# Hybrid attention encoder block: another order of stores, fetches and product parts around the routed units, and q's rotary copies issued by ScalarE

## The reference

```python
h = rmsnorm(x, norm_mix)
qa, ka, va, ga, cq, ckv, kr, gb = split(h @ w_in)
ya = window_attention(qa, ka, va, sink) * silu(ga)      # group A: banded, 8 heads
q = (rmsnorm(cq) @ w_uq)      # 8 heads of 64 plain + 32 rotary columns
kv = (rmsnorm(ckv) @ w_ukv)   # 8 heads of 64 (k) + 64 (v); one rotary k for all heads
yb = latent_attention(q, k, v) * silu(gb)               # group B: dense, 8 heads
out = final_norm * rmsnorm(x + concat(ya, yb) @ w_out)
```

## Time and profile before

| What | Value |
|---|---|
| Time, median of 3 runs | 622.18 us (621.98 to 623.96) |
| The profiled execution | 621.12 us, its span 619.3 us |
| PE busy | 601.3 us, 97% of the span |
| DVE busy | 446.7 us, 72% |
| ACT busy | 357.3 us, 58% |
| POOL busy | 288.4 us, 47% |
| Granted PE clock, mean | 0.997 of full speed |

### The profile page before, as it was taken

How to read it: one execution, slowest core, us unless ns; L and a number is a source line. 1 busy time by engine, 2 the same in 40 slices (tenths; PEclk the granted TensorE clock), 3 DMA queues, 4 the chain that set the end, 5 groups by cost and what they waited for, 6 DMA issues and landing times.

```text
span 619.3 us, 9200 instructions
## 1 busy us (share of the span) xinstructions
PE 601.3 (97%) x3092; PEld 485.7 (78%) x3092; DVE 446.7 (72%) x804; ACT 357.3 (58%) x762; POOL 288.4 (47%) x269
## 2 busy tenths in 40 slices
PE   8999999999999999999999999898989989999996
PEld 7888887888888888888887777676766767888885
DVE  5776653334445258999997899787887878799884
ACT  6645232313335147888785868677777778543563
POOL 4610705406657234354546626675666666320601
PEclk9999999999999999999999999999999999999999
DMA  6688458684767510101108656658567554499043
GB/s 248 187 278 246 125 151 288 203 272 135 256 209 275 172 35 1 35 7 29 26 22 236 165 135 170 162 135 211 129 168 191 128 147 146 156 355 350 3 152 121
DMA packets 70990, 100.00 MB, mean 161 GB/s; under 512 B 10072, under 2 KB 41824, under 8 KB 70944
## 3 DMA queue, kind: packets, MB, share of 16 engines
q1 hardware_dynamic: 70784, 99.15, 53.2%
q10 hardware_dynamic: 160, 0.27, 0.1%
HBM read 59.12 MB, written 30.57 MB: 145 GB/s over the span
## 4 chain that ended last, share of the span: by engine, by line
PE 77%; DMA 7%; DVE 5%; POOL 4%; SPq 3%; ACT 3%; issue 1%; POOLq 0%; ACTq 0%
PE ps L1817 17%; PE ps L1819 17%; PE ps L1818 17%; PE ps L2089 4%; DMA p_land<-probs_scratch 4%; PE ps L1989 3%; PE ps L2108 3%; PE ps L2109 2%; PE ps L2019 2%; PE ps L2024 2%; PE ps L1999 2%; PE ps L1976 2%; PE ps L1975 2%; PE ps L2000 1%; DVE pT_lo L1667 1%
## 5 line engine op out<-in xcount | busy, mean ns | idle before, releaser
L1667 DVE TENSOR_TENSOR pT_lo<-ps,pT_hi 128x512 fp32r<-128x512 f32 x106 | 71.7, 688 | 35.6 <-ACT pT_hi L1232 35.3
L1817 PE MATMUL ps<-hT_hi,w_hi 128*128 128x512 f32 x208 | 84.0, 404 | 0.0
L1219 ACT ACTIVATE p_b<-ps,stat 128x1024 f32<-128x1024 f32 x64 | 71.3, 1115 | 17.5 <-DVE stat L1644 16.6
L1819 PE MATMUL ps<-hT_hi,w_lo 128*128 128x512 f32 x208 | 81.4, 391 | 0.0
L1818 PE MATMUL ps<-hT_lo,w_hi 128*128 128x512 f32 x208 | 81.1, 390 | 0.0
L1644 DVE TENSOR_REDUCE stat<-ps 128x1 f32<-128x1024 f32 x64 | 76.7, 1214 | 2.2 <-PE ps L2039 2.0
L1232 ACT ACTIVATE pT_hi<-ps 128x512 fp32r<-128x512 f32 x106 | 62.3, 595 | 22.6 <-PE ps L2089 22.2
L2089 PE MATMUL ps<-ident,p_b 128*128 128x128 f32 x424 | 65.5, 278 | 2.0 <-DVE pT_lo L1667 1.9
L2089 PEld LDWEIGHTS ps<-ident,p_b 128*128 128x128 f32 x424 | 50.2, 141 | 22.0 <-DVE pT_lo L1667 6.5
L2108 PE MATMUL ps<-pT_hi,vB 128*128 128x512 f32 x128 | 55.8, 436 | 7.7 <-POOL pT_lo L924 7.7
L2109 PE MATMUL ps<-pT_lo,vB 128*128 128x512 f32 x128 | 51.0, 398 | 0.0
(11 more groups left out here) (222 smaller groups left out, 1482.8 us busy)
## 6 DMA issues: line engine op xcount, KB each, us to landing
w_raw<-w_in SPq DMA_DIRECT2D x13, 512.0 KB, 4.4
probs_scratch<-p_blk SPq DMA_DIRECT2D x44, 128.0 KB, 2.9
p_land<-probs_scratch SPq DMA_DIRECT2D x11, 512.0 KB, 4.7
x_in<-x SPq DMA_DIRECT2D x8, 512.0 KB, 3.8
wt_raw<-w_out SPq DMA_DIRECT2D x8, 512.0 KB, 4.3
t_scratch<-wt_hi SPq DMA_DIRECT2D x16, 256.0 KB, 2.6
t_scratch<-wt_lo SPq DMA_DIRECT2D x16, 256.0 KB, 2.8
q<-q_h SPq DMA_DIRECT2D x16, 256.0 KB, 4.0
```

The costliest lines, as they stand in the source:

```text
L1219: nc.scalar.activation(p_b[:, (U + 1) % 4, :], ps[:, b:b + 2, :].rearrange("p b c -> p (b c)"), ACT.Exp, bias=nm_b[:, U % 4:U % 4 + 1], ac ...
L1667: nc.vector.tensor_tensor(pT_lo[at_], ps[:, 4 + a, :].rearrange("p (k c) -> p k c", c=P), f(pT_hi[at_]), ALU.subtract).then_inc(s_bTl, 1)
L1817: nc.tensor.matmul(o, a_hi, b_hi, start=first, stop=False, skip_group_check=goes_on)
L1819: return nc.tensor.matmul(o, a_lo, b_hi, start=False, stop=last, skip_group_check=goes_on)
```

## The change

On SP, `copy_k_rows` goes ahead of `store_probs`, `copy_q_c` leaves SP for all heads from 2 on, and the fetch of the second routed unit of a head goes ahead of the fetch of reciprocals. On POOL, `routed_lo` goes ahead of the pieces, and the pieces of a head are taken as (0 and 3), 1, 2, 4, 5, none, none, 7. On ACT, `copy_q_c` is issued behind the first exponential of the pairs 10, 18, 26, 34, 42 and 50, and both parts of `routed_hi` stand behind the last `pT_b_hi` of the pair. On PE, the parts of the product move: part 0 to the end of the pair with U % 4 = 2, parts 1 and 2 in the next pair, part 3 to the very start of the pair after it.

```diff
@@ SP
                 copy_q_rows(h)
                 store_recips(2 * h - 3)
+                copy_k_rows(h)
                 store_probs(U)
                 fetch_recips(2 * h - 3)
-                copy_k_rows(h)
                 fetch_probs(U)
-                copy_q_c(h, s_dup)
                 if h + 1 < HEADS:
                     load_qk(h + 1)
                 store_recips(2 * h - 2)
                 if U + 4 in ROUTED:
                     store_probs(U + 4)
+                    fetch_probs(U + 4)
                 fetch_recips(2 * h - 2)
-                if U + 4 in ROUTED:
-                    fetch_probs(U + 4)
@@ POOL
             for U in range(B_UNITS + 8):
-                if U // NT + 1 < HEADS:
-                    split_piece(U // NT + 1, U % NT)
                 if U - 5 in ROUTED:
                     routed_lo(U - 5)
+                if U // NT + 1 < HEADS:
+                    for i in ((0, 3), (1,), (2,), (4,), (5,), (), (), (7,))[U % NT]:
+                        split_piece(U // NT + 1, i)
@@ ACT
+            def copy_q_c(h):
+                act.wait_ge(s_sph, 2 * h - 1)
+                for i in range(4):
+                    tiles = f(q_h[HD:QK, :]).rearrange("p (a b c) -> p a b c", b=2, c=P)[:, :, i // 2, :]
+                    nc.scalar.dma_start(f(q_c[h % 2][i * ROPE:(i + 1) * ROPE, :]).rearrange("p (a c) -> p a c", c=P),
+                                        tiles).then_inc(s_dup, 16)
...
                 exp_b(U)
+                if U >= NT and U % NT == 2 and U // NT + 1 < HEADS:
+                    copy_q_c(U // NT + 1)
                 if U >= 2:
                     pT_b_hi(U - 2, 1)
                     pT_b_hi(U - 1, 0)
                 exp_b(U + 1)
-                if U - 4 in ROUTED:
-                    routed_hi(U - 4, 0)
                 if U >= 2:
                     pT_b_hi(U - 1, 1)
                 if U - 4 in ROUTED:
-                    routed_hi(U - 4, 1)
+                    for a in range(2):
+                        routed_hi(U - 4, a)
@@ PE
+                G = (U - 6) // 4
+                if U >= 10 and U % 4 == 2:
+                    pv_b(G - 1, 3)
                 full_b(U)
                 rope_b(U)
                 gated_last(beside_b[1])
                 turn_b(U - 2, 0)
                 full_b(U + 1)
                 turn_b(U - 2, 1)
-                if U >= 6:
-                    pv_b((U - 6) // 4, (U - 6) % 4)
+                if U >= 6 and U % 4 == 0:
+                    pv_b(G, 1)
                 gated_last(beside_b[2])
                 turn_b(U - 1, 0)
-                if U >= 6:
-                    pv_b((U - 6) // 4, (U - 5) % 4)
+                if U >= 6 and U % 4 == 0:
+                    pv_b(G, 2)
                 gated_last(beside_b[3])
                 turn_b(U - 1, 1)
+                if U >= 6 and U % 4 == 2:
+                    pv_b(G, 0)
...
+                if U == B_UNITS:
+                    pv_b((U - 6) // 4, 1)
```

## The result

The changed kernel takes 639.87 us (median; 638.79 to 641.60) against 622.62 for the kernel before: a ratio of 1.029 with an interval of 1.026 to 1.032. It is slower by 17 us. The forecast was 631.5, in a range up to 636.5: the direction is right, about half of the size is missing, and the time lies outside the range. The profiled execution took 639.61 us, its span 637.8.

The account below looks back on a forecast made before the run. PE, busy 97% of the span, was taken as the bound. Terms +0.7 (pair 6), +4.7 (8 to 50), +2.2 (52 to 60), +1.7 (behind) gave +9.3 on 621.12: 630.4, forecast as a 631.5 us median; range 620.5 to 636.5.

Parts of the forecast that it names:

- The gain on the routed groups: Pairs 8 to 50: waits for routed units, queue order on SP and POOL, all go; worth 9.9 us.
- PE's order: Latent attention pairs: routed groups 0.5 us dearer, short 4.64, long 7.32; unrouted groups 1.7 dearer, 6.8 and 7.06.
- The chain of rotary product, maximum and two exponentials: Routed short pairs: chain sums to 4.64 us against 4.28 of PE work, so PE waits 0.36 in each.
- The last block of an unrouted short pair: On PE: waits 1.7 us for DVE to free its bank, starting 4.33 behind the rotary product.
- Where the issues begin: ACT, pairs 10 to 50 with copies: issues can't begin before the first exponential does, by the standalone wait's stamp.
- hidden copies: Rival, 20%: ACT's sequencer issues the copies ahead, so their 9.6 us vanish and the time is 621.9.
- What the issues cost: ACT, six pairs with copies: 2.65 us of issues, 1.10 covered by the exponential; 1.6 us per head, 9.6 in all.
- The clock: Rival, 9%: granted clock falls after PE's waits, 1.4 us beyond each wait; two to five falls make 634 to 638.
- the likeliest case: The forecast itself, 55%: copies, PE's order and gain sum to +9.3 us, giving 631.5.
- the rival in which the change doesn't do what it says: Rival, 6%: q_c's transfers make the stores of probabilities late; the old 7.7 us of waits return: 639.

Follow-up runs that it names:

- e2: Kernel before with only the new order of SP, POOL and ACT's routed copies; q_c copies on SP, PE's order as before: 614.53 us, ratio 0.989.
- e7: e2 with part 0 of a routed group behind the first block of the last unit instead of ahead of it: 612.08 us, ratio 0.984.
- e8: e2 with ACT's two routed conversions around the pair's last copy as before, so only SP's and POOL's orders are new: 612.32 us, ratio 0.984.
- e5: Changed kernel with ACT's four q_c issues directly ahead of the pair's first exponential instead of behind it: 623.62 us, ratio 1.002.
- e1: Changed kernel with the q_c copies back on SP, behind fetch_probs(U), and none on ACT: 620.74 us, ratio 1.000.
- e12: Changed kernel with PE's waits filled by 8 added products of zeros ahead of the rotary product that waits: 632.47 us, ratio 1.018.
- e9: Changed kernel with PE's six long waits filled by 16 products of zeros ahead of the rotary product that waits: 638.16 us, ratio 1.027.
- e11: Kernel before with the q_c copies moved to ACT and all else as before: 630.59 us, ratio 1.015.
- e10: e7 and e8 together: SP's and POOL's new orders, routed part 0 behind the last unit's first block, ACT's order as before: 612.24 us, ratio 0.985.
- e4: Changed kernel with PE's order as in the kernel before, the q_c copies staying on ACT: 622.7 us, ratio 1.003.
- e3: Kernel before with only the PE part of the change, its new order: 627.8 us, ratio 1.012.

## Where the prediction held, and the steps that failed

**The gain on the routed groups** holds: PE has no wait for POOL's pT_lo, and e2, with nothing else in it, is 1.1% faster. Of the 9.9 us put on it, e2 brings 5.6 (136.1 to 130.5) and e7 8.2; the rest goes with waits that the old order of PE leaves. That the waits were one of queue order on SP and POOL, read from the chain, is shown by e8.

**PE's order** holds nearly to the number: short pairs of 4.66 (4.64 forecast), long ones of 7.22 (7.32), unrouted ones of 6.72 and 6.96 (6.8 and 7.06). The chain of rotary product, maximum and two exponentials was summed from durations in rows of before, and the sum held. The last block of an unrouted short pair waits for DVE, as said, but less. Pair 58 in the changed kernel's timeline, which answers to the earlier trace rows:

```profile
531.73 1.29 DVE L1674 TENSOR_TENSOR pT_lo<-ps,pT_hi 128x512 fp32r<-128x512 f32 x2
532.47 0.66 PE L2096 MATMUL ps<-ident,p_b 128*128 128x128 f32 x4 [1.07 <-DVE pT_lo L1674]
```

The block starts when the first of these two low halves is out. PE waits 1.07 us for it, where 1.7 were written, and the block starts 4.29 behind the rotary product (528.18), where 4.33 were.

**Where the issues begin** was right: in all six pairs with the first exponential, which the stamp of the standalone wait had told. The Trainium skill (Advanced Engine Details and Errata, Sequencer Loop) was read for the opposite case, issues that are over before the exponential. e5 bears out its rule for an engine that is merely busy; for an instruction whose semaphore hasn't come, the 24 issues of the changed kernel speak against it. The prediction left open whether the standalone wait itself is held in the queue; the L1212 of the changed kernel, stamped 2.6 us ahead of the exponential, answers that for the wait on the maximum. The 20% on hidden copies stood on the half of the rule that fails here.

**What the issues cost** is the first step that failed, by size alone: 12.1 us (e1), not 9.6. The term is "2.65 us of issues, of which the exponential covers 1.10", the same for all six heads; it took SP's row for ACT. The issues' own line in the changed kernel (minimum, median and maximum of one, in ns), and its timeline in pair 34:

```profile
L1244 ACTq DMA_DIRECT2D q_c<-q_h x24: 592/625/1493, 366.8 to 504.8; - x24
```

```profile
448.17 2.12 ACTq L1244 DMA_DIRECT2D q_c<-q_h  x2
450.31 1.28 ACTq L1244 DMA_DIRECT2D q_c<-q_h  x2
```

The median agrees with SP's (2.63 / 4), and pairs 18 and 50, whose four issues took 2.6 and 2.7 us, grew by 1.7 each, close to the 1.6 of the forecast. But in pairs 10 and 34 one of the four took 1.36 and 1.49 us, and these pairs grew by 2.4 to 2.5; in pairs 26 and 42 the four took 2.9 us, and the pairs grew by 1.9. Why single issues take so long is open. SP issued nothing during the two longest, and in e12 pair 34 had none such.

**The clock** is the step that made the forecast too low: the likeliest case put six waits of PE of 1.96 us into its sum and put what follows them at nothing. The runs showed 6.6 us there, of the 8.4 that are missing in pairs 8 to 50. It was there as a rival, at the right price (1.4 us; measured 1.32) and with five falls in its range, but at 9%, apart from the likeliest case and added to it only for two falls. The row of pair 22 had shown one fall behind one wait, and the likeliest case put six waits of almost 2 us into the same stage. Those could not be 9% apart from it. How many falls there would be, the rows before didn't tell: of the five waits for POOL one was followed by one, and it wasn't the longest. The 2.3 us that the prediction put before pair 24 lie in pair 38, which kept the full clock; the wait of pair 22 was 2.1 us.

```profile
448.01:455.76 7.75, 5.50 (x29) 3.82 (x28) 4.33 (x6) 5.18 (x10) 3.01 (x3) 1.00 0.87 216
```

At that rate six waits make one fall, about 1.4 us more, and not five. e9 and e12 show that in this order the fall comes of PE's wait: the same order and the same late exponential, with PE kept at work, and none of twelve pairs is slowed. That holds beyond the traces: the four executions of the changed kernel had a mean clock of 0.983 to 0.985, the eight of e9 and e12 one of 0.995 to 0.999.

**What stays open** is which wait does it. In the changed kernel the wait of pair 18 (6.31 long) was followed by a fall and that of pair 50 (6.35) not; in e11 the longest of all, 3.3 us, was followed by none. What PE did in the pair ahead of the wait differs between the two orders, and no run tried to vary that. The kernel before varies too: its mean clock was 0.987 to 0.997 over the executions in which these runs were measured against it, and the profiled one, with its single fall in group B, is at the top of that range. So part of what e2, e7, e8 and e10 gain may be falls that no longer come (their mean clock was 0.995 to 1.000).

In pairs 8 to 50 the terms add up: 4.7 forecast, + 2.5 (the issues), - 0.8 (e1's 130.4 where the sum without copies was 131.2), + 6.6 (the clock) = 13.0, against 13.1 measured.

One number was met by luck: the rival in which the change doesn't do what it says gave 639, next to the measured 639.9. Its mechanism, the old waits of PE for POOL come back, isn't there at all.

## What to carry to other kernels

An issue on a compute engine costs what it takes away from that engine's chain, so look for the place at which the engine waits for another anyway: the same four issues cost 12.1 us (and the clock's 6.6) behind the exponential and 3.7 us (134.1 - 130.4) ahead of it. Where a change puts gaps into PE's work, and a row of the trace shows a lower clock behind such a gap, put its price times the falls to be expected into the likeliest sum, and let the range take in a fall behind every gap: here five of six came, where the kernel before had shown one in five. And when a change is made of several orders at once, run them apart: here one of three was worth 1.1 to 1.6%, and the other two ate it up.

## What the runs showed of the hardware

- A transfer's issue on ACT took 0.59 to 1.49 us, median 0.63; the four ran one behind the other, with ACT's other work beside them only where that stood ahead in the program.
- ACT's sequencer issued transfers while the engine was busy with earlier instructions (386.76 against 387.50 in e5), and in 24 of 24 cases of the changed kernel not before an exponential that lacked its input had begun.
- After waits of PE of 1.8 to 2.7 us, behind the copies, the granted clock of the next pair was 0.78 to 0.80 in 6 of 12 cases (the changed kernel and e4), for 1.32 us more: part of the pair ran at the lower of the two levels, 1.2 instead of 2.4 GHz (0.50 from 400.3 to 403.5 in pair 20). In e11, with waits of up to 3.3 us, it was 1.00 in 6 of 6. With the wait filled by products of zeros it was 1.00 in 12 of 12. Without any copy on ACT it was 0.81 in pair 22 before and 0.83 in pair 54 of e3. Each of these counts is of one execution.
